# An encoder step on one core: score maxima of the first three tiles ahead of gating, and a tail that begins with the convolution's products

## The chip, the cores and the metric

The kernel runs on one core of a Trainium2 chip. The metric is the device time of one execution in microseconds (us); the time before is the median of three executions.

## The reference

One layer of a streaming encoder reads 2048 prompt frames and 64 sample frames of 1024 channels. Cut to what matters:

```python
h = rmsnorm(x, norm_g)
proj = h @ w_in                                  # 1024 x 2832, all groups at once
q, k = rmsnorm(aq, q_g), rmsnorm(ak, k_g)        # 8 query heads, 2 key heads, width 64
y_attn = band_attention(q, k, v, sinks) * silu(ag)   # chunks of 64, band of 192, ALiBi, sinks
o, state = gla_chunked(gq, gk, gv, log_sigmoid(glr @ w_up + b) / 16)
y_gla = rmsnorm(o, gla_g) * silu(gg)
c = depthwise_conv31(cv * sigmoid(cgl)) + conv_b
y_conv = (silu(layernorm(c)) @ w_pw + b_pw) * silu(cg)
y = concat([y_attn, y_gla, y_conv]) @ w_out
return x + y, new key and value windows, GLA state, conv state
```

All of it is float32. Each large product is made of three products of rounded parts: high by high, high by low and low by high.

## The kernel before

Every engine has a queue of its own, in program order, and the engines meet at semaphores. The order in each queue is written out by hand. Pass A runs over 17 tiles of 128 frames (`t.n` from 0 to 16; the last is the sample) and does attention with its part of the output; pass B runs over 8 blocks of 256 frames and does the gated linear attention, the convolution and their part of the output. The change touches pass A's `body_a` on each engine for the tiles 0 to 2 (`OPENING` holds the tiles 0 and 1), and pass B's end.

Weights come from DRAM as 24 pieces of the input projection and 8 of the output (`A.pieces`, `3 * KT` is the first of the output). ScalarE rounds each to its high part (`split_hi`, L479), VectorE takes the rest as its low part (`split_lo`, L489 for the input, L492 for the output). There are four buffers for the output pieces, so the last four (`3 * KT + STAGES` on) are loaded while tile 0 is worked on. On SyncE's queue these loads stand behind the token load of tile 3 (L531), which waits until ScalarE has squared the tokens of tile 2 (`norm_square`, L650).

In a tile of pass A, TensorE transposes the normalised q and k (L2222), projects part of the next tile (L779), transposes the gates into the bank `T[1]` (L2242), makes scores in two banks (L2257; the third and fourth pair wait for maxima of the first and second), projects on, transposes the softmax (L2292 and L2301), makes the output of the tile before (L795) and the product with v (L2315 to L2317). VectorE takes the low parts of q and k (L1632, L1568) and of v (L1640, two inputs from SBUF), the product of the gate's tanh with the gate (L1655), the maxima of scores plus bias (`scores_max`, L1591), the negatives (L1597), the low part of the x of tile t + 2 (L706), the softmax's sum (L1692) and scale. It gates the output (`y_gate`, L1558), of which ScalarE takes the high part (`y_hi_half`, L1264) and VectorE the low (`y_lo_half`, L1537). For tiles 0 and 1 gating and parts come in the next tile's turn, ahead of its maxima. ScalarE evacuates the projections (L720), takes high parts (L1143, L1272, L1157), the tanh (L1161) and the exponentials (L1184).

The reciprocal norm of x goes a long way: the square on ScalarE, mean and power on GpSimd (`norm_rinv`), a transpose on TensorE into `T[1]` (`spread_rinv`, L668), a copy on ScalarE (`take_rinv`, L673), and GpSimd's multiplication of the x of that tile for pass B (`norm_x`, L679). GpSimd also makes the powers of the norm of q and k (`qk_rinv`, L1005) out of VectorE's sums (`qk_square`, L1578 and L1580).

At the end of pass B, for the last block, VectorE gates the convolution's activation (L1882), updates the GLA state (`state`, L1969), sums the squares of o (L1811), adds the convolution's gate (`y_conv`, L1891) and normalises o (L1829), after GpSimd's power (L1056). ScalarE takes the high part of the convolution's half of y (L1399), VectorE the low (L1848). TensorE transposes o (`o_T`, L2424) and makes four banks of output (`output_end`, L2407) of 12 products each, half from the convolution, half from the GLA group; VectorE adds the residual (L1983), and SyncE stores.

Of the kernel before, what the change touches and what calls it, by code (L numbers as in the profile page):

```python
# [24 lines left out]
ALU = mybir.AluOpType  # L25
# [180 lines left out]
def build(nc, ins, consts, x_T, outs):  # L206
# [13 lines left out]
    with es:  # L220
# [774 lines left out]
        def _(pool):  # L995
# [11 lines left out]
            def body_a(t):  # L1007
# [6 lines left out]
                when(t + 2, norm_rinv)  # L1014
                n = t + 1
                if t.real():
# [6 lines left out]
                    if (t + 2).real():  # L1023
                        pool.wait_ge(x_wide, t.n + 3)
                    else:
                        pool.wait_ge(n_rinv, t.n + 1)
                        pool.wait_ge(x_normed, TILES)
# [6 lines left out]
                if n.real() and n.n > 0:  # L1034
                    qk_rinv(n)
                if n.n == LAST:
# [67 lines left out]
        def _(act):  # L1104
# [9 lines left out]
            def body_a(t):  # L1114
# [23 lines left out]
                if t.real():  # L1138
# [13 lines left out]
                    if t.n == 0:  # L1152
                        take_rinv(t1)
                        act.wait_ge(n_step, 4)
                        evacuate(t1, 0, raw[:, 0:512], bank_of("in", t1.n, 0)[:, :])
# [3 lines left out]
                    act.wait_ge(gate_psum, t.n + 1)  # L1159
                    need(act, y_gated, 2 * t.n)  # L1160
                    nc.scalar.activation(gth[:, :], T[1][:, :], ACT.Tanh, scale=0.5).then_inc(gate_tanh, 1)  # L1161
                    if t.n == 0:
                        split_hi(A, 3 * KT + 2, 3 * KT + STAGES)
                    act.wait_ge(v_lo, t.n + 1)
# [3 lines left out]
                if t.n - 1 in OPENING:  # L1168
                    y_hi_half(t + -1, 0)
                if (t + -1).real():  # L1170
# [35 lines left out]
                if t.real():  # L1206
                    exp_scores(0)
                    exp_scores(1)
                if t.n == LAST:
# [4 lines left out]
                if t.n == 1:  # L1214
                    split_hi(A, 3 * KT + STAGES, len(A.pieces))
                if t.n == 0:
                    norm_square(t + 2)
# [21 lines left out]
                if t.n in OPENING:  # L1239
                    pT_hi(1)  # L1240
                if t1.real():
# [9 lines left out]
                if t.n >= 0:  # L1251
# [262 lines left out]
        def _(dve):  # L1514
# [68 lines left out]
            def body_a(t):  # L1583
# [35 lines left out]
                if t.fixed and t.n == -1:  # L1619
# [3 lines left out]
                    split_lo(A, 2 * KT + STAGES, 2 * KT + STAGES + 2)  # L1623
                    qk_square(B0)
                    split_lo(A, 2 * KT + STAGES + 2, 3 * KT)
# [16 lines left out]
                if t.n - 1 in OPENING:  # L1642
                    y_gate(t + -1, 0)
                    y_gate(t + -1, 1)
                    y_lo_half(t + -1, 0)
                if (t + -1).real():
                    y_lo_half(t + -1, 1)
                if t.real():
# [5 lines left out]
                    dve.wait_ge(gate_tanh, t.n + 1)  # L1654
# [1060 lines left out]
```

## Time and profile before

| | before |
|---|---|
| median of 3 runs | 931.96 us (931.54 to 934.63) |
| profiled execution | 932.18 us, span 930.4 us |
| mean granted TensorE clock | 0.991 |
| TensorE busy | 895.2 us, 96% of the span |
| TensorE weight load busy | 803.9 us, 86% |
| VectorE busy | 783.1 us, 84% |
| ScalarE busy | 481.1 us, 52% |
| GpSimd busy | 215.8 us, 23% |

The span runs from the first to the last instruction of the profiled execution; its own time is 1.8 us longer, for what lies around the span. Busy shares are averages over stages with different limits. In rows, PE is TensorE, PEld its weight load, DVE VectorE, ACT ScalarE, POOL GpSimd and SP SyncE; L12 is line 12 of the kernel before. In rows in order of time the brackets at the end hold the idle time of the engine just before the instruction, and what ended it. Instructions that follow without a gap are merged into one row, with their count.

### The profile page before, as it was taken

How to read it: one execution, taken by the hardware profiler on the slowest of the kernel's cores; microseconds unless marked ns; L12 is line 12 of the kernel's file. 1: busy time of each engine (PE TensorE's matmuls, PEld its weight loads, DVE VectorE, ACT ScalarE, POOL GpSimd, SP SyncE). 2: the span in 40 equal slices, each digit the busy share in tenths (PEclk: the TensorE clock that was granted, in tenths of full speed). 3: DMA queues.
4: the chain of work that ended last, by engine and by line, in shares of the span. 5: the costliest groups of instructions: out<-in, count | busy, mean ns of one | idle time of the engine just before them, and what ended most of it. 6: DMA issues, size and time to landing. Idle time of an engine off the chain costs nothing. (4 is left out here: it accounts for less than half of the span.)

```text
span 930.4 us, 15888 instructions
## 1 busy us (share of the span) xinstructions
PE 895.2 (96%) x5655; PEld 803.9 (86%) x5655; DVE 783.1 (84%) x1896; ACT 481.1 (52%) x1182; POOL 215.8 (23%) x259
## 2 busy tenths in 40 slices
PE   6889999999999999998999999999999999999997
PEld 5777888888888888886998888889999899998985
DVE  6878888888888888889879999888788969788983
ACT  7676667667776666668663261341515224151331
POOL 1432222222221222223022231311202021120310
PEclk9999999999999999999999999999999999999999
DMA  8551322223233333234451221121130302203021
GB/s 285 202 192 69 114 98 108 90 104 114 103 114 114 113 114 98 73 119 135 126 161 51 76 69 63 52 80 57 40 98 1 116 23 69 69 26 111 1 80 59
DMA packets 58062, 88.04 MB, mean 95 GB/s; under 512 B 10080, under 2 KB 34528, under 8 KB 57984
## 3 DMA queue, kind: packets, MB, share of 16 engines
q1 hardware_dynamic: 57984, 87.03, 28.5%
q8 instruction: 45, 0.74, 0.3%
q14 instruction: 33, 0.27, 0.1%
HBM read 60.47 MB, written 26.60 MB: 94 GB/s over the span
## 5 line engine op out<-in xcount | busy, mean ns | idle before, releaser
L1798 DVE SCALAR_TENSOR_TENSOR acc<-ub,cwh,acc 128x256 f32<-128x256 f32 (+1 forms) x480 | 230.3, 539 | 1.5 <-ACT acc L1308 0.7
L779 PE MATMUL J<-whi,xhi 128*128 128x512 f32 (+1 forms) x400 | 148.0, 371 | 7.7 <-DVE wlo L489 7.7
L2200 PE MATMUL J<-xbh,whi 128*128 128x256 f32 (+1 forms) x512 | 152.4, 298 | 0.1
L2200 PE MATMUL J<-xbl,whi 128*128 128x256 f32 (+1 forms) x512 | 146.9, 289 | 1.5 <-DVE xbl L587 1.5
L2200 PE MATMUL J<-xbh,wlo 128*128 128x256 f32 (+1 forms) x512 | 147.7, 289 | 0.0
L779 PE MATMUL J<-wlo,xhi 128*128 128x512 f32 (+1 forms) x400 | 143.4, 359 | 0.0
L779 PE MATMUL J<-whi,xlo 128*128 128x512 f32 (+1 forms) x384 | 137.9, 362 | 0.0
L2200 PEld LDWEIGHTS J<-xbh,whi 128*128 128x128 f32 x512 | 98.8, 193 | 2.2 <-DVE wlo L489 0.8
L2200 PEld LDWEIGHTS J<-xbl,whi 128*128 128x128 f32 x512 | 98.8, 194 | 1.7 <-issue 1.7
L2200 PEld LDWEIGHTS J<-xbh,wlo 128*128 128x128 f32 x512 | 99.0, 193 | 0.5
L779 PEld LDWEIGHTS J<-whi,xhi 128*128 128x128 f32 x400 | 77.5, 194 | 17.8 <-DVE xlo L699 7.2
L779 PEld LDWEIGHTS J<-wlo,xhi 128*128 128x128 f32 x400 | 77.8, 194 | 9.2
L779 PEld LDWEIGHTS J<-whi,xlo 128*128 128x128 f32 x384 | 74.3, 194 | 11.2
L1184 ACT ACTIVATE sc<-sc,nmx 128x192 f32<-128x192 f32 x132 | 58.6, 446 | 9.0 <-DVE nmx L1597 9.0
L795 PE MATMUL J<-whi,yhi 128*128 128x512 f32 x136 | 56.2, 413 | 0.9 <-DVE wlo L492 0.9
L1591 DVE CUSTOM_DVE_ANT_0 sc<-S,bias,sinks 128x192 f32<-128x192 f32 (+2 forms) x132 | 48.8, 406 | 6.3 <-PE S L2257 6.1
L795 PE MATMUL J<-wlo,yhi 128*128 128x512 f32 x136 | 53.1, 390 | 0.0
L679 POOL TENSOR_TENSOR xraw<-xraw,rb 128x1024 f32<-128x1024 f32 x17 | 41.4, 2433 | 43.3 <-ACT rb L673 43.3
L795 PE MATMUL J<-whi,ylo 128*128 128x512 f32 x128 | 50.1, 392 | 0.0
L1056 POOL TENSOR_TENSOR orr<-oms,mhalf 128x8 f32<-128x8 f32 (+1 forms) x9 | 17.8, 1980 | 136.4 <-DVE oms L1821 136.4
L2257 PEld LDWEIGHTS S<-kT,qT 128*128 128x128 f32 x264 | 33.6, 191 | 9.0 <-DVE mx L1591 5.4
L2257 PE MATMUL S<-kT,qT 128*128 128x192 f32 x264 | 35.5, 274 | 6.0 <-DVE mx L1591 4.1
(287 smaller groups left out, 2244.5 us busy)
## 6 DMA issues: line engine op xcount, KB each, us to landing
out<-res SPq DMA_DIRECT2D x60, 256.0 KB, 2.0
x_normed_scratch<-xraw SPq DMA_DIRECT2D x17, 512.0 KB, 2.9
xtok<-in_x_prompt SPq DMA_DIRECT2D x16, 512.0 KB, 3.6
res<-in_x_prompt SPq DMA_DIRECT2D x16, 512.0 KB, 4.5
xraw<-xT SPq DMA_DIRECT2D x15, 512.0 KB, 3.5
xbraw<-x_normed_scratch SPq DMA_DIRECT2D x14, 512.0 KB, 5.0
res<-out SPq DMA_DIRECT2D x14, 512.0 KB, 4.2
wraw<-in_w_in SPq DMA_DIRECT2D x52, 128.0 KB, 2.5
```

Source lines behind the costliest of these rows:

```text
L679: nc.gpsimd.tensor_tensor(xraw[t.par][:, :, :], xraw[t.par][:, :, :], rb[:, :].unsqueeze(1).to_broadcast([P, KT, P]), ALU.mult).then_inc(x ...
L779: last = nc.tensor.matmul(bank[:, 0:width], x[x_slot(ps, t)][:, k, :], w, start=(k == 0 and n == 0), stop=(k == KT - 1 and n == len(produc ...
L795: last = nc.tensor.matmul(bank[:, :], y[:, k, :], w, start=(k == 0 and n == 0), stop=(k == 3 and n == len(products) - 1))
L1056: nc.gpsimd.tensor_tensor(orr[rows, a:e], oms[rows, a:e], mhalf[rows, a:e], ALU.pow).then_inc(go_r, 1)
L1184: last = nc.scalar.activation(unit(u), unit(u), ACT.Exp, bias=nmx[:, u:u + 1], accum_out=esum[:, u:u + 1])
L1591: nc.vector.tensor_tensor_reduce(out=unit(u)[:, cols], in0=S[n % 2][:, c * BAND:(c + 1) * BAND][:, cols], in1=bias[:, n, cols], scale=1.0, ...
L1798: nc.vector.scalar_tensor_tensor(acc[:, j, 0:frames], src, w, acc[:, j, 0:frames], ALU.mult, ALU.add).then_inc(conv_step, 1)
L2200: last = nc.tensor.matmul(bank[:, 0:w], wt, x[:, k, 0:w], start=(k == 0 and m == 0), stop=(k == KT - 1 and m == 2))
L2257: last = nc.tensor.matmul(S[n % 2][:, c * BAND:(c + 1) * BAND], qT[:, n, c, :, :].rearrange("p e q -> p (e q)"), band(t, n // 2, o, c), st ...
```

## The change

In VectorE's queue, the gate product of the tiles 0 to 2 moves behind the maxima and the sink difference. The gating of the tile before moves behind the second negatives in the tiles 1 and 2, and the low halves of its output move behind the gate product. The last four output weights, which stood together in tile 1, are spread: one ahead of the maxima, one behind the second negatives, two behind the gate product. The squares of q and k of tile 0 move one input weight ahead.

In ScalarE's queue, v's high part goes ahead of the reciprocal row and of the evacuation of q in tile 0; the reciprocal row of tile 2 is taken in tile 1, behind v's high part. The tanh and both high halves of the tile before move behind the first two pairs of exponentials in the tiles 1 and 2. The last four output weights stand two ahead of v's copies and two behind the high halves. The square of tile 2's tokens moves behind the second half of the softmax's high parts.

In GpSimd's queue, the reciprocal norm of tile 2 moves behind v's copies and the powers for q and k of tile 1; the copies wait for the multiplication of tile 1's x instead. On TensorE the transpose of tile 2's reciprocal norm moves behind the whole product with v.

At the tail, the last state update moves behind the sums and means of the squares of o, and the output begins with the first two products of each of the convolution's two parts in the first bank, ahead of the transposes of o; three banks instead of two have their convolution half made ahead of the GLA half.

```diff
@@ GpSimd, body_a
-                when(t + 2, norm_rinv)
+                if t.n != 0:
+                    when(t + 2, norm_rinv)
...
-                    if (t + 2).real():
+                    if t.n == 0:
+                        pool.wait_ge(x_normed, 2)
+                    elif (t + 2).real():
                         pool.wait_ge(x_wide, t.n + 3)
...
                 if n.real() and n.n > 0:
                     qk_rinv(n)
+                if t.n == 0:
+                    norm_rinv(t + 2)
@@ ScalarE, body_a
-                    if t.n == 0:
-                        take_rinv(t1)
-                        act.wait_ge(n_step, 4)
-                        evacuate(t1, 0, raw[:, 0:512], bank_of("in", t1.n, 0)[:, :])
                     act.wait_ge(*taken(t, 1))
                     nc.scalar.activation(vcat[t.par][:, :, 0:HD], raw[:, 640:768].rearrange("p (h d) -> p h d", d=HD),
                                          ACT.Copy).then_inc(v_hi, 1)
-                    act.wait_ge(gate_psum, t.n + 1)
-                    need(act, y_gated, 2 * t.n)
-                    nc.scalar.activation(gth[:, :], T[1][:, :], ACT.Tanh, scale=0.5).then_inc(gate_tanh, 1)
+                    if t.n in (0, 1):
+                        take_rinv(t1)
+                    if t.n == 0:
+                        act.wait_ge(n_step, 4)
+                        evacuate(t1, 0, raw[:, 0:512], bank_of("in", t1.n, 0)[:, :])
+
+                    def tanh_of_gate():
+                        act.wait_ge(gate_psum, t.n + 1)
+                        need(act, y_gated, 2 * t.n)
+                        nc.scalar.activation(gth[:, :], T[1][:, :], ACT.Tanh, scale=0.5).then_inc(gate_tanh, 1)
+
+                    if t.n - 1 not in OPENING:
+                        tanh_of_gate()
...
+                    if t.n == 1:
+                        split_hi(A, 3 * KT + STAGES, 3 * KT + STAGES + 2)
...
-                if t.n - 1 in OPENING:
-                    y_hi_half(t + -1, 0)
-                if (t + -1).real():
+                if (t + -1).real() and t.n - 1 not in OPENING:
                     y_hi_half(t + -1, 1)
...
                     exp_scores(0)
                     exp_scores(1)
+                if t.n - 1 in OPENING:
+                    tanh_of_gate()
+                    y_hi_half(t + -1, 0)
+                    y_hi_half(t + -1, 1)
+                if t.n == 1:
+                    split_hi(A, 3 * KT + STAGES + 2, len(A.pieces))
...
-                if t.n == 1:
-                    split_hi(A, 3 * KT + STAGES, len(A.pieces))
-                if t.n == 0:
-                    norm_square(t + 2)
...
                 if t.n in OPENING:
                     pT_hi(1)
+                if t.n == 0:
+                    norm_square(t + 2)
...
-                if t.n >= 0:
+                if t.n > 0:
                     when(t + 2, take_rinv)
@@ VectorE, body_a
-                    split_lo(A, 2 * KT + STAGES, 2 * KT + STAGES + 2)
+                    split_lo(A, 2 * KT + STAGES, 2 * KT + STAGES + 1)
                     qk_square(B0)
-                    split_lo(A, 2 * KT + STAGES + 2, 3 * KT)
+                    split_lo(A, 2 * KT + STAGES + 1, 3 * KT)
...
-                if t.n - 1 in OPENING:
-                    y_gate(t + -1, 0)
-                    y_gate(t + -1, 1)
-                    y_lo_half(t + -1, 0)
-                if (t + -1).real():
+                if (t + -1).real() and t.n - 1 not in OPENING:
                     y_lo_half(t + -1, 1)
+                if t.n == 1:
+                    split_lo(A, 3 * KT + STAGES, 3 * KT + STAGES + 1)
...
-                    dve.wait_ge(gate_tanh, t.n + 1)
-                    nc.vector.scalar_tensor_tensor(gth[:, :], gth[:, :], 1.0, T[1][:, :], ALU.add,
-                                                   ALU.mult).then_inc(gate_ready, 1)
+                    if t.n > 2:
+                        gate_product()
                     scores_max(0)
...
                     scores_neg(1)
+                    if t.n - 1 in OPENING:
+                        y_gate(t + -1, 0)
+                        y_gate(t + -1, 1)
+                    if t.n == 1:
+                        split_lo(A, 3 * KT + STAGES + 1, 3 * KT + STAGES + 2)
...
+                    if t.n <= 2:
+                        gate_product()
+                if t.n == 1:
+                    split_lo(A, 3 * KT + STAGES + 2, len(A.pieces))
+                if t.n - 1 in OPENING:
+                    y_lo_half(t + -1, 0)
+                    y_lo_half(t + -1, 1)
...
-                if t.n == 1:
-                    split_lo(A, 3 * KT + STAGES, len(A.pieces))
@@ VectorE, end of pass B
-                    state(b, 1)
                     o_sums(g)
                     o_means(g)
+                    state(b, 1)
@@ TensorE, body_a
-                when(t + 2, spread_rinv)
+                if t.n != 0:
+                    when(t + 2, spread_rinv)
                 if t.n > 1:
                     out(1)
                 if t.real():
                     pv(1)
+                if t.n == 0:
+                    spread_rinv(t + 2)
@@ TensorE, output_end
+                first = empty_bank("out", b, 0)
+                pe.wait_ge(yc_hi, groups_before(b + 1))
+                output_half(first, 0, 0, (2, 3), parts=(0, 1))
                 o_T(groups(b)[0])
                 pe.wait_ge(yc_lo, groups_before(b + 1))
-                for s in (0, 1):
+                output_half(first, 0, 0, (2, 3), parts=(2,))
+                for s in (1, 2):
                     output_half(empty_bank("out", b, s), s // 2, s % 2, (2, 3))
                 pe.wait_ge(yg_lo, groups_before(b + 1))
-                for s in (0, 1):
+                for s in (0, 1, 2):
                     output_half(bank_of("out", b, s), s // 2, s % 2, (0, 1)).then_inc(slot_done, 1)
-                for s in (2, 3):
-                    output_half(empty_bank("out", b, s), s // 2, s % 2, (2, 3, 0, 1)).then_inc(slot_done, 1)
+                output_half(empty_bank("out", b, 3), 1, 1, (2, 3, 0, 1)).then_inc(slot_done, 1)
```

`output_half` takes a new argument `parts`, which of the three products to make; without it, it makes all three.

## Rows read from the trace of the kernel before

**Rows 1.** Windows of 25 us: busy time by engine, granted clock (PEclk), DMA.

```profile
50.00:75.00 25.00, 21.47 (x117) 17.65 (x118) 20.55 (x59) 19.02 (x50) 6.49 (x8) 0.93 0.39 139
...
100.00:125.00 25.00, 24.95 (x146) 21.65 (x145) 21.11 (x56) 17.00 (x45) 6.50 (x8) 1.00 0.31 106
```

**Rows 2.** Waits of TensorE, 30 to 60 us: total, times, longest (us).

```profile
PE T L2222 <- DVE qkn L1735: 2.1, 1, 2.1
```

**Rows 3.** The same, 60 to 80 us.

```profile
PE S L2257 <- DVE mx L1591: 1.4, 2, 1.3
PE S L2257 <- issue: 1.1, 1, 1.1
PE J L795 <- DVE wlo L492: 0.9, 1, 0.9
```

**Rows 4.** The same, 80 to 100 us.

```profile
PE S L2257 <- DVE mx L1591: 1.3, 2, 1.1
```

**Rows 5.** Windows of one microsecond; the columns of Rows 1.

```profile
34.00:35.00 1.00, 1.00 (x7) 1.00 (x6) 0.95 (x2) 0.97 (x2) 0.00 (x0) 0.50 0.77 78
69.00:70.00 1.00, 1.00 (x3) 0.76 (x3) 0.93 (x2) 1.00 (x3) 0.00 (x0) 0.50 0.49 197
95.00:96.00 1.00, 1.00 (x6) 0.79 (x6) 0.86 (x7) 1.00 (x3) 0.00 (x0) 1.00 1.00 410
916.00:917.00 1.00, 1.00 (x3) 0.75 (x3) 0.43 (x1) 0.00 (x0) 0.00 (x0) 0.50 0.00 0
```

**Rows 6.** VectorE by time: start, us, what, wait before and its releaser.

```profile
28.16 1.41 DVE L489 SCALAR_TENSOR_TENSOR wlo<-res,gain,whi 128x512 fp32r<-128x512 f32 x2
...
39.06 1.81 DVE L1640 TENSOR_TENSOR vcat<-raw,vcat 128x128 fp32r<-128x128 f32 x1 [1.04 <-ACT vcat L1157]
...
48.47 0.30 DVE L1692 TENSOR_TENSOR den<-esum,esink 128x8 f32<-128x8 f32 x1 [1.43 <-ACT esink L1227]
...
60.89 0.29 DVE L1640 TENSOR_TENSOR vcat<-raw,vcat 128x128 fp32r<-128x128 f32 x1
...
63.90 0.76 DVE L1537 TENSOR_TENSOR ylo<-osum,yhi 128x256 fp32r<-128x256 f32 x2 [2.05 <-ACT yhi L1264]
64.69 0.69 DVE L1655 SCALAR_TENSOR_TENSOR gth<-gth,T 128x512 f32<-128x512 f32 x1
65.30 0.41 DVE L1591 CUSTOM_DVE_ANT_0 sc<-S,bias,sinks 128x192 f32<-128x192 f32 x1
...
69.16 1.23 DVE L706 TENSOR_TENSOR xlo<-xraw,xhi 128x1024 fp32r<-128x1024 f32 x1
70.31 2.49 DVE L492 TENSOR_TENSOR wlo<-wraw,whi 128x512 fp32r<-128x512 f32 x4
```

**Rows 7.** GpSimd in order of time.

```profile
38.33 2.40 POOL L679 TENSOR_TENSOR xraw<-xraw,rb 128x1024 f32<-128x1024 f32 x1 [4.89 <-ACT rb L673]
```

**Rows 8.** ScalarE in order of time.

```profile
45.02 1.05 ACT L650 ACTIVATE xtok<-xtok 128x1024 f32<-128x1024 f32 x1
...
54.98 0.59 ACT L1202 ACTIVATE olo<-S 64x512 f32<-64x512 f32 x1 [1.72 <-PE S L2317]
...
58.42 1.16 ACT L1272 ACTIVATE kT<-T 64x128 fp32r<-64x128 f32 x4
```

**Rows 9.** SyncE's DMA issues in order of time.

```profile
46.18 0.33 SPq L531 DMA_DIRECT2D xtok<-in_x_prompt  x1
...
47.03 1.88 SPq L455 DMA_DIRECT2D wraw<-in_w_out  x4
```

**Rows 10.** The wraw buffer's loads issued from 40 to 72 us.

```profile
DMA to landing us min/median/max: 5.3/5.8/6.1
```

**Rows 11.** TensorE at the tail, in order of time.

```profile
913.60 0.66 PE L2424 MATMUL T<-ident,on 128*128 128x128 f32 x4 [2.44 <-DVE on L1829]
```

**Rows 12.** VectorE at the tail.

```profile
909.02 1.15 DVE L1969 SCALAR_TENSOR_TENSOR stp<-stp,dec,T 32x64 f32<-32x64 f32 x4
```

**Rows 13.** ScalarE at the tail.

```profile
912.10 0.63 ACT L1399 ACTIVATE ybc<-cl 128x512 fp32r<-128x512 f32 x1 [3.24 <-DVE cl L1891]
```

More of the change, by code:

```diff
@@ L1641, in body_a, with gate_product @@
                                             f(vcat[t.par][:, :, 0:HD]), ALU.subtract).then_inc(v_lo, 1)
-                if t.n - 1 in OPENING:
-                    y_gate(t + -1, 0)
-                    y_gate(t + -1, 1)
-                    y_lo_half(t + -1, 0)
-                if (t + -1).real():
-                    y_lo_half(t + -1, 1)
+                if (t + -1).real() and t.n - 1 not in OPENING:
+                    y_lo_half(t + -1, 1)
+                if t.n == 1:
+                    split_lo(A, 3 * KT + STAGES, 3 * KT + STAGES + 1)
+                def gate_product():
+                    dve.wait_ge(gate_tanh, t.n + 1)
+                    nc.vector.scalar_tensor_tensor(gth[:, :], gth[:, :], 1.0, T[1][:, :], ALU.add,
+                                                   ALU.mult).then_inc(gate_ready, 1)
                 if t.real():
@@ L2388, in output_end, with output_half @@
             def output_end(b):
+                first = empty_bank("out", b, 0)
+                pe.wait_ge(yc_hi, groups_before(b + 1))
+                output_half(first, 0, 0, (2, 3), parts=(0, 1))
                 o_T(groups(b)[0])
                 pe.wait_ge(yc_lo, groups_before(b + 1))
-                for s in (0, 1):
+                output_half(first, 0, 0, (2, 3), parts=(2,))
+                for s in (1, 2):
                     output_half(empty_bank("out", b, s), s // 2, s % 2, (2, 3))
                 pe.wait_ge(yg_lo, groups_before(b + 1))
-                for s in (0, 1):
+                for s in (0, 1, 2):
                     output_half(bank_of("out", b, s), s // 2, s % 2, (0, 1)).then_inc(slot_done, 1)
-                for s in (2, 3):
-                    output_half(empty_bank("out", b, s), s // 2, s % 2, (2, 3, 0, 1)).then_inc(slot_done, 1)
-            def output_half(bank, i, h, ks, first=2):
+                output_half(empty_bank("out", b, 3), 1, 1, (2, 3, 0, 1)).then_inc(slot_done, 1)
+            def output_half(bank, i, h, ks, first=2, parts=(0, 1, 2)):
                 for k in ks:
@@ L2405, in output_half @@
                     high, low = i * P, y_low_at(i * P)
-                    for m, (at, wt) in enumerate(((high, hi), (high, lo), (low, hi))):
+                    for m in parts:
+                        at, wt = ((high, hi), (high, lo), (low, hi))[m]
                         last = nc.tensor.matmul(bank[:, :], y[:, k % 2, at:at + P], wt,
```

## Prediction

> **What bounds the kernel now.** I read the windows first, then TensorE's waits in the stretches that are not full, then each engine in order of time there and at the tail. The windows show where time can be had at all: from 50 to 75 us TensorE is busy 21.47 of 25 us, from 100 to 125 us 24.95 [rows 1]. Later TensorE is the bound, so that what is won before 100 us is kept to the end: the loads and all engines there follow TensorE's progress. The waits of the first stretches name VectorE nearly every time: 2.1 us for the normalised q and k of tile 0 [rows 2], in tile 1 1.4 us for score maxima, 1.1 before the scores and 0.9 for the last output weight [rows 3], in tile 2 1.3 us for maxima [rows 4].
>
> The single microseconds show a second loss. At 34, 69 and 916 us the granted clock is 0.50, TensorE's lower level of 1.2 GHz [rows 5]. These came after its waits of 2.1 us [rows 2], of 1.4 us in two pieces [rows 3] and of 2.4 us [rows 11]; after the 1.3 us of tile 2 the clock was full at 95 us [rows 4, 5]. The price is in the mean of the 25 us that hold the second one, 0.93 [rows 1]: 25 x 0.07 = 1.75 us of TensorE's work, if TensorE sets the pace then.
>
> VectorE's order in time shows why tile 1 waits: 60.89 low half of v, then gating of tile 0's output, a wait of 2.05 us for ScalarE's high halves of y, their low halves, the gate product, and only at 65.30 the first score maximum [rows 6]. It ended the last of four output weights at 72.80 (70.31 + 2.49) [rows 6], and TensorE's first output product waited for that [rows 3].
>
> **The change, step by step.**
>
> *Tile -1.* The squares of q and k go ahead of one of two weights that stood before them. One such weight takes 1.41 / 2 = 0.7 us [rows 6]. GpSimd's powers, the normalised q and k and TensorE's transposes follow 0.7 sooner. TensorE's wait of 2.1 can take it [rows 2]. The weight that steps back is late by less than this and the next one, for which TensorE waited anyway, is as early as before. Ends: 0, if GpSimd's power is drawn out by VectorE's weights beside it, and 0.7. I take 0.7.
>
> *Tile 0.* Four moves: v's copy goes ahead of the reciprocal norm and of tile 1's q on ScalarE; VectorE's gate product goes behind the maxima; GpSimd copies v before tile 2's norm; and ScalarE's square of tile 2's tokens, 1.05 us plus a short read of the sum [rows 8], leaves the place between the first and second pair of exponentials. The softmax sum on VectorE waited 1.43 us for ScalarE [rows 6], so it comes about 1.0 sooner (at most 1.43, at least 0 if VectorE itself is late). The square now stands ahead of the evacuation of tile 1's gates; behind these ScalarE waited 1.72 us for TensorE [rows 8], which covers it. Sum at tile 1's start: 1.7. Tile 2's reciprocal row moves out of ScalarE's way too, behind v's copy: some 0.3 more for tile 1's keys, so 2.0.
>
> *The queue behind the moved square.* SyncE's token load for tile 3 waits for that square, and behind it stand the residual of tile 0 and the last four output weights: token load at 46.18, first weight at 47.03 [rows 9]. ScalarE went idle at 54.98 - 1.72 = 53.26 [rows 8], after the evacuation of the gates, which I take as long as the copy at 54.98, 0.6; the square comes ahead of it and all is 1.7 sooner, so it ends near 53.26 - 0.6 - 1.7 + 1.15 = 52.1, and the first weight is issued near 53.0. Landing took 5.3 to 6.1 us [rows 10]: 58.3 to 59.1. That is where ScalarE now asks for it.
>
> *Tile 1.* From the start of v's low half to the first maximum there are now 65.30 - 60.89 = 4.4 us [rows 6]. Between them there will be only one weight, 2.49 / 4 = 0.6 [rows 6], but also a new wait. ScalarE's keys end at 59.58 now [rows 8], hence about 57.6; v's high half and the reciprocal row add 0.6, and GpSimd then multiplies tile 2's x from 58.2 on for 2.40 us [rows 7], to 60.6. VectorE comes to v's low half at 60.89 - 2.0 = 58.9. In tile 0 the same instruction, with GpSimd's multiplication beside it, took 1.81 us and ended at 40.87, just after the multiplication's 40.73; alone it took 0.29 [rows 6, 7]. So I count it to end at 60.8, and the first maximum at about 61.45, or 3.85 sooner. From there to the last weight VectorE took 72.80 - 65.30 = 7.5 us [rows 6]. Now two gatings (as long as the low halves of y, 0.76), the gate product (0.69) and the low halves (0.76) come in, 2.2; the first weight (0.6) and x's low half (1.23) go out, 1.8 [rows 6]. So y is ready at about 61.45 + 7.9 = 69.3, 3.5 sooner than 72.80. ScalarE's tanh, its high halves and the last weights lie a little ahead of these by the same count.
>
> TensorE then has nothing for about 2.9 us (its second half of the gates' projection ends near 66.4 by my estimate: maxima 3.85 sooner, 1.4 of waits gone). That is longer than the 2.1 that came before a slow stretch [rows 2, 5], so I count one, 1.7 us. The present one at 69 us is in part hidden by the 0.9 that TensorE waited after it [rows 3]. Sum at tile 2's start: 3.5 - 1.7 = 1.8. Ends: 0, if the new order holds VectorE or ScalarE up by as much as it frees, and 3.5.
>
> The Trainium skill, GPSIMD Engine Reference, section Specifications, says that GpSimd shares its SBUF interfaces with VectorE and contends with VectorE instructions that have two SBUF inputs. It does not say that the later one waits for the other's end; if the two only halved each other's rate, v's low half would take an estimated 0.6 and all behind it would come 1.3 sooner, a time of 926.9. By the row of tile 0 it waits for the end, and by that goes the sum.
>
> *Tile 2.* The same order without weights: both waits for maxima go, 1.3 [rows 4]. VectorE's gate product and low halves then come while TensorE projects the next tile. Ends: 0, if the softmax is late by as much, and 1.3. Sum: 3.1.
>
> *Tail.* VectorE's state update of 1.15 us [rows 12] steps behind the sums of squares, so GpSimd's root and the normalised o come earlier; TensorE no longer waits for these first. It begins the output with four products of the convolution half as soon as ScalarE has its high half, at 912.10 + 0.63 = 912.73 [rows 13]; now it begins at 913.60 with the transposes [rows 11]. All that follows has its inputs by then (the transposes come after four products, the gated part after 14 more), so TensorE runs through: 0.8 sooner. The slow stretch at 916 [rows 5] stays, since a wait of about 1.6 us is left ahead. The last bank, its addition and its store are as now. Ends: 0.4, if the clock rises when it does now, and 2.5, if it does not fall.
>
> *Sum.* 1.8 + 1.3 + 0.8 = 3.9 us from the profiled execution's 932.18 (its span is 930.4), which is 0.2 over the median of the runs: 932.18 - 3.9 = 928.3, and 928.2 with the median in mind. About 0.3%, 2.8 us, is what a measurement of this kernel can tell from no change: below 929.2 is faster, above 934.8 slower.
>
> **Rivals.**
>
> *The clock does not fall in tile 1* (or v's low half isn't held up), 0.22: for it, 1.3 us of waits in tile 2 left the clock up [rows 4, 5]; against it, 2.9 is longer than any of these. The 1.7 stay: 926.5.
>
> *Tile 1 gives back what tile 0 won,* 0.20: VectorE's work ahead of the first output product isn't less than before, only in another order, and each engine hands over to another some ten times. Where ScalarE's high halves come late, VectorE stands behind them with the low halves and the softmax, and TensorE with the output. Then only tile 2 and the tail are left, 2.1: 930.1.
>
> *The tail alone,* 0.07: the maxima weren't what held TensorE, the softmax was: 931.4.
>
> *Slower, through late weights,* 0.04: VectorE's split of the first of the last four weights stands ahead of tile 1's first maximum, ScalarE's half of it ahead of v's copies and all exponentials. By the count it is wanted split by 60.8, so landed by 60.2, and lands by 59.1: 1.1 to spare. Each microsecond more costs one. To end above 934.8 it would have to eat the 3.9 and 2.8 more, landing near 67, 14 us after its issue, where 6.1 was the longest [rows 10]. A landing one or two microseconds late ends in the second rival.
>
> **How the numbers follow.** My forecast, 927.2 to 929.4, has 0.47. The likeliest time is 928.2. The range reaches from 926.0 (clock up in tile 1, and part of the tail's) to 930.6 (tile 1 giving all back, and a little of tile 2): about 0.1 is left out on each side. Faster: 0.45 of the forecast, the 0.22 and nothing of the rest, 0.67. Slower: 0.04, and 0.01 for what I don't see, 0.05. Same: 0.28.
>
> **What would show it.** Right: first transposes of tile 0 near 32.0 instead of 32.7; the softmax sum of tile 0 near 46.6; v's low half of tile 1 near 1.9 us long; first maximum near 61.5; one TensorE wait of 2 to 3 us ahead of the first output product, with clock 0.50 behind it; no waits for maxima in tile 2; output at the tail from 912.8 less what was won before. Wrong: ScalarE waiting for a weight's DMA in tile 1, a wait of TensorE for the softmax in tile 0 or 1 that isn't there now, or a span that is shorter only behind 900 us.

## Result and profile after

The changed kernel took 925.15 us, the median of four runs (925.01 to 925.71), against 931.86 for the kernel before beside it: a ratio of 0.9929, 95% interval 0.9912 to 0.9946. So it is 6.7 us faster (5.0 to 8.2 by the interval), where 3.9 were forecast, and it ends 0.85 us below the range. A second measurement later gave 0.9929 again (0.9916 to 0.9941). The profiled execution took 925.71 us, with a span of 923.9 (930.4 before).

TensorE's waits after the change, in the stretches of [rows 2 to 4] (waited for: us in total, times, longest):

```profile
PE T L2270 <- ACT rb L673: 1.3, 2, 0.8
PE T L2250 <- DVE qkn L1763: 1.3, 1, 1.3
PE S L2285 <- DVE kT L1583: 0.6, 1, 0.6
...
PE J L795 <- DVE ylo L1552: 2.4, 1, 2.4
...
PE S L2343 <- DVE px L1741: 0.5, 1, 0.5
```

The wait for the normalised q and k is 1.3 us in place of 2.1. In tile 1 the three waits have become the one of 2.4 us ahead of the first output product, and tile 2 has none for maxima. The single microseconds that answer to [rows 5] (busy us of each engine, then the granted clock, DMA share, GB/s; the output at the tail is now at 909 to 912):

```profile
34.00:35.00 1.00, 0.82 (x7) 0.58 (x6) 0.39 (x1) 0.93 (x4) 0.00 (x0) 1.00 0.48 53
69.00:70.00 1.00, 1.00 (x4) 0.81 (x3) 0.45 (x3) 0.46 (x4) 0.00 (x0) 0.50 0.00 0
95.00:96.00 1.00, 1.00 (x10) 0.91 (x8) 0.97 (x3) 0.82 (x3) 0.00 (x0) 1.00 0.00 0
...
911.00:912.00 1.00, 1.00 (x6) 0.79 (x5) 0.30 (x2) 0.63 (x1) 0.00 (x0) 1.00 0.00 0
```

Two of the three slow stretches (granted clock 0.50) are gone, at 34 us and at the tail; the one in tile 1 is still there. Each of the two profiles has two more in the middle, near 440 and 529 us before and near 416 and 526 us after, which the forecast did not look at. VectorE, GpSimd and ScalarE in order of time, where [rows 6 to 8] stood:

```profile
45.38 0.16 DVE L1720 TENSOR_TENSOR den<-esum,esink 128x8 f32<-128x8 f32 x1
...
57.75 1.94 DVE L1655 TENSOR_TENSOR vcat<-raw,vcat 128x128 fp32r<-128x128 f32 x1
...
60.32 0.42 DVE L1606 CUSTOM_DVE_ANT_0 sc<-S,bias,sinks 128x192 f32<-128x192 f32 x1
...
67.09 0.76 DVE L1552 TENSOR_TENSOR ylo<-osum,yhi 128x256 fp32r<-128x256 f32 x2
```

```profile
57.15 2.39 POOL L679 TENSOR_TENSOR xraw<-xraw,rb 128x1024 f32<-128x1024 f32 x1 [4.75 <-ACT rb L673]
```

```profile
57.35 1.29 ACT L479 ACTIVATE whi<-wraw 128x512 fp32r<-128x512 f32 x2 [0.28 <-DMA wraw<-in_w_out]
```

v's low half takes 1.94 us and ends at 59.69, just after GpSimd's multiplication (57.15 + 2.39 = 59.54). ScalarE waits 0.28 us for a weight. At the tail, TensorE before (the row ahead of [rows 11]), then after:

```profile
909.16 1.99 PE L2468 MATMUL T<-cth,params 128*128 128x256 f32 x8 [1.23 <-DVE cth L1882]
```

```profile
905.17 1.99 PE L2503 MATMUL T<-cth,params 128*128 128x256 f32 x8 [1.23 <-DVE cth L1910]
908.89 0.47 PE L2442 MATMUL J<-whi,ybc 128*128 128x512 f32 x1 [1.72 <-ACT ybc L1414]
...
909.89 0.60 PE L2459 MATMUL T<-ident,on 128*128 128x128 f32 x4
```

Cut at six of TensorE's own instructions, every trace gives a ledger of the span. "Start" ends at tile 0's transposes of q and k, "tile 0" at those of tile 1, "1a" at tile 1's first output product, "1b" at tile 2's transposes, "tile 2" at tile 3's; "middle" runs to the last block's products of `cth` (the convolution's gated activation), "tail" from there to the end. An asterisk marks a slow stretch (left out in the middle).

```
kernel                     start  tile 0    1a     1b    tile 2  middle   tail
before                     32.73  23.10*  17.11*  8.47   27.04   800.71  21.21*
before, again (e1)         32.63  21.81   17.11  10.00*  27.09   800.80  21.21*
squares only (e13)         31.74  21.83   17.11   8.43   27.06   801.39  21.21*
changed                    31.09  21.60   15.26  10.03*  25.71   801.48  18.75
changed, again (e10)       31.70  21.61   15.26   8.79   26.00   802.22  18.75
head only (e2)             31.75  21.59   15.24   9.97*  25.70   801.99  21.21*
```

In the profiled execution of before the stretch of tile 1 lies in 1a, which takes the same 17.11 us without it; in the other three that have one there it comes behind the first output product, in 1b, where it costs 1.2 to 1.6 us.

### The profile page after: what moved, and what is told of

It is laid out like the page before. It is cut to its first block and busy times, and to the rows that moved or that the text cites. A ratio compares the mean times of both kernels' runs of the same rounds, so it can differ in the third digit from the quotient of the medians.

```text
span 923.9 us, 15888 instructions
## 1 busy us (share of the span) xinstructions
PE 890.1 (96%) x5655; PEld 800.9 (87%) x5655; DVE 784.4 (85%) x1896; ACT 481.6 (52%) x1182; POOL 215.7 (23%) x259
## 5 line engine op out<-in xcount | busy, mean ns | idle before, releaser
L2389 PE MATMUL J<-whi,xbh 128*128 128x272 f32 x136 | 40.0, 294 | 0.0
L2389 PE MATMUL J<-whi,xbl 128*128 128x272 f32 x136 | 39.3, 289 | 0.0
```

The source lines that it names most:

```text
L2389: last = nc.tensor.matmul(bank[:, 0:B.widths[1]], x[:, k, at:at + P], wt, start=(k == 0 and m == 0), stop=(k == KT - 1 and m == 2))
```

## Experiments

**The kernel before once more (e1), the head alone (e2), the tail alone (e3).** e2 is the changed kernel with the tail of before, e3 the kernel before with the changed tail: the state update one place later, and

```diff
+                first = empty_bank("out", b, 0)
+                pe.wait_ge(yc_hi, groups_before(b + 1))
+                output_half(first, 0, 0, (2, 3), parts=(0, 1))
                 o_T(groups(b)[0])
...
```

> The kernel before, profiled once more. Theory A (the first loads fell otherwise in the two executions): the powers of tile 0's q and k, the wait for its first transposes (32.73 and 31.09 us in the two profiles) and the end of GpSimd's first multiplication differ by some tenths between two profiles of this same kernel too, up to 0.9. Theory B (the reordering gave all 1.6 us): first transposes within 0.2 of 32.73. For the clock: if slow stretches belong to the waits, they lie at 34, 68 and 914 us again.

> The change without its two edits at the tail. Theory A (the tail gave 2.5, since a slow stretch of the clock went with it): 4.0 to 4.4 us under the kernel before, 927.5 to 927.9, and a slow stretch at the tail as before. Theory B (the tail gave the 0.8 of its earlier start, the rest lies in the first tiles): 5.9 under, 926.0.

> The kernel before with the two edits at the tail alone. Theory A: 2.5 us under the kernel before, 929.4, with no slow stretch behind 900 us. Theory B: 0.8 under, 931.1, and the slow stretch still there.

e1 took 932.44 us, e2 928.39 (0.9950, 0.9936 to 0.9964), e3 929.83 (0.9969, 0.9958 to 0.9981), beside 932.66. Theory A of e2 and of e3 holds: e2 keeps the slow stretch at the tail, e3 has none there. Head 4.3 and tail 2.8 us add up to 7.1, the whole being 6.7; within the intervals the two gains simply add. e1, the same program as before, shows what the forecast had no view of:

```profile
32.63 0.63 PE L2222 MATMUL T<-ident,qkn 128*128 128x128 f32 x4 [2.11 <-DVE qkn L1735]
...
71.55 0.47 PE L795 MATMUL J<-whi,yhi 128*128 128x512 f32 x1 [2.50 <-DVE wlo L492]
71.86 0.57 PE L795 MATMUL J<-wlo,yhi 128*128 128x512 f32 x1
72.22 0.63 PE L795 MATMUL J<-whi,ylo 128*128 128x512 f32 x1
```

```profile
46.85 0.17 DVE L1692 TENSOR_TENSOR den<-esum,esink 128x8 f32<-128x8 f32 x1 [0.44 <-ACT esink L1227]
```

```profile
34.00:35.00 1.00, 1.00 (x11) 1.00 (x10) 0.97 (x2) 0.95 (x3) 0.00 (x0) 1.00 0.00 0
...
73.00:74.00 1.00, 1.00 (x4) 0.74 (x3) 1.00 (x5) 0.71 (x3) 0.00 (x0) 0.50 0.00 0
```

The same wait of 2.11 us is not followed by half clock at 34 us this time. TensorE, faster in tile 0 and 1, then waits 2.50 us for the last weight and not the 0.92 of [rows 3], and the slow stretch comes behind that, where a product takes 0.63 us in place of 0.39. The sum of tile 0, 1a and 1b is 48.68 us in the one, 48.92 in the other. The first transposes come within 0.1 us of 32.73, as theory B had it; but e3, e5 and e6, with the same head, have them at 31.56, 32.25 and 32.22, so the spread of theory A is there too.

**What the tail is worth without its products (e6), and the clock without the tail's order (e5).** e6 is the kernel before with the state update alone moved, e5 the kernel before with

```diff
             def output_end(b):
+                first = empty_bank("out", b, 0)
+                for n in range(9):
+                    nc.tensor.matmul(first[:, :], xbh[:, n % KT, 0:P], whi[:, W_OUT:W_OUT + 512], ...)
```

> The kernel before with the last state update behind the sums and means of the squares of o, and the output's order as before. Theory A (any work of TensorE that begins some 0.8 us sooner leaves the clock up): 0.8 to 2.5 under the kernel before. Theory B (what counts is the four products ahead of the transposes): 0.0 to 0.8 under, since the transposes of o, and with them all products, begin when o is normalised, about 912.7 instead of 913.6; the slow stretch stays.

> The kernel before, with nine products of finished operands added on TensorE in the output, ahead of the transposes of o (their results are overwritten; the order of all else is that of before). TensorE then does something in the 2.4 us in which it waited for o. Theory A (the tail's gain in the changed kernel is for the larger part the slow clock stretch behind that wait, worth 1.7 us): the granted clock stays at 1.00 behind the place, the last products end 1.7 us sooner although no work was moved, and the time is 1.2 to 2.0 us under the kernel before, a ratio of 0.9979 to 0.9987. Theory B (the gain is the earlier start of the output): no gain, a ratio of 1.000 or a little above, with the slow stretch there or not.

e6: 929.93 us (0.9977, 0.9967 to 0.9986). e5: 930.56 (0.9981, 0.9971 to 0.9991). TensorE in e6, then in e5:

```profile
908.63 1.99 PE L2468 MATMUL T<-cth,params 128*128 128x256 f32 x8 [1.23 <-DVE cth L1882]
912.19 0.66 PE L2424 MATMUL T<-ident,on 128*128 128x128 f32 x4 [1.57 <-DVE on L1829]
912.98 0.53 PE L2407 MATMUL J<-whi,ybc 128*128 128x512 f32 x1
913.32 0.62 PE L2407 MATMUL J<-wlo,ybc 128*128 128x512 f32 x1
```

```profile
911.02 2.44 PE L2392 MATMUL J<-whi,xbh 128*128 128x512 f32 x9
913.81 0.66 PE L2428 MATMUL T<-ident,on 128*128 128x128 f32 x4 [0.35 <-DVE on L1829]
914.41 0.50 PE L2411 MATMUL J<-whi,ybc 128*128 128x512 f32 x1
914.75 0.39 PE L2411 MATMUL J<-wlo,ybc 128*128 128x512 f32 x1
```

From the `cth` products to the transposes e6 needs 3.56 us where the kernel before needs 4.44, and its products still take 0.62: its tail is 20.53 us, 0.7 shorter. e5 moves nothing, its transposes come 4.43 us behind `cth`, its products take 0.39, and its tail is 19.67 us, 1.5 shorter. So theory A of e5 holds: at the tail the clock is the larger part. One thing stays open: by the times e6 gains nearly as much as e3 (0.9977 and 0.9969, overlapping). Its profiled execution, 930.95 us, had a mean clock of 0.993; seven of its twelve runs had 0.994, which is about one slow stretch less (e9 with one has 0.998, e15 with none 1.000), and took 929.6 to 930.0. If that was the stretch at the tail, moving the state update is enough to be rid of it in most executions; whether the four products ahead of the transposes are needed is not shown.

**The squares of q and k (e4, e13), and the clock of tile 0 (e14).** e4 undoes that move in the changed kernel, e13 makes it alone in the kernel before, e14 adds nine products ahead of tile 0's transposes in the kernel before.

```diff
-                    split_lo(A, 2 * KT + STAGES, 2 * KT + STAGES + 2)
+                    split_lo(A, 2 * KT + STAGES, 2 * KT + STAGES + 1)
                     qk_square(B0)
-                    split_lo(A, 2 * KT + STAGES + 2, 3 * KT)
+                    split_lo(A, 2 * KT + STAGES + 1, 3 * KT)
```

> The changed kernel with one edit undone: VectorE's squares of q and k of tile 0 stand behind two weights again, as before the change. Theory A (the move of the squares is worth what TensorE waited less there, 2.1 us of the kernel before against 1.3 of the changed one; the rest of the 1.64 us by which the changed kernel's first transposes came sooner is how the first loads happened to land): TensorE's wait for the normalised q and k is 2.1 us again, and the time is 0.7 to 0.9 us above the changed kernel's, a ratio to the kernel before of 0.9932 to 0.9942. Theory B (the whole 1.64 us came of the move): 1.6 us above it, a ratio of 0.9942 to 0.9950. Theory C (what tile 0 wins is swallowed by the waits of tile 1, as in my second rival): no difference, 0.9925.

> The kernel before with one edit of the change alone: VectorE's squares of q and k of tile 0 ahead of one weight. Theory A (the shorter wait of 1.4 us instead of 2.1 leaves TensorE's clock up, and both are kept): first transposes of tile 0 near 31.4 us, no slow stretch between 31 and 38 us, 21.8 us from them to those of tile 1, and the time 0.7 to 2 us under the kernel before, a ratio of 0.978 thousandths short of one at most: 0.9978 to 0.9992. Theory B (in the old order tile 1 gives back what the clock saves in tile 0: of five executions with the old head tile 1 took 27.1 us in the two with a fast tile 0 and 25.6 in two of the three with a slow one): only the 0.7 of the shorter wait is left or not even that, 0.9990 to 1.0000.

(The range meant there is 0.9978 to 0.9992; the figure ahead of it is a slip.)

> The kernel before, with nine products of finished operands added on TensorE ahead of tile 0's transposes, in the 2.1 us of the wait for the normalised q and k (results overwritten; nothing is moved). Theory A (the slow stretch at 34 us is a cost of its own, 1.3 us of tile 0): no slow stretch there, tile 0 takes 21.8 us in place of 23.1, and the time is 0.5 to 1.3 us under the kernel before, 0.9986 to 0.9995. Theory B (tile 1 gives it back, in its wait for the last weights): tile 0 takes 21.8 us, tile 1 27.1, and the time is that of the kernel before, 0.9995 to 1.0003.

e4: 926.55 us (0.9936, 0.9919 to 0.9952), start 32.15, wait 2.11, a slow stretch back at 33 to 36 us: theory A, though the interval of the ratio holds all three. e13: 930.22 us (0.9985, 0.9976 to 0.9994), a gain of 1.4 us, as theory A had it. Its trace:

```profile
31.74 0.63 PE L2222 MATMUL T<-ident,qkn 128*128 128x128 f32 x4 [1.41 <-DVE qkn L1735]
...
53.57 0.63 PE L2222 MATMUL T<-ident,qkn 128*128 128x128 f32 x4
...
70.68 0.47 PE L795 MATMUL J<-whi,yhi 128*128 128x512 f32 x1 [2.50 <-DVE wlo L492]
70.98 0.40 PE L795 MATMUL J<-wlo,yhi 128*128 128x512 f32 x1
```

The wait is 1.41 and tile 0 at full clock; here even the 2.50 us in tile 1 leave the clock up (0.40 a product). e14: 931.08 us (0.9989, 0.9979 to 0.9999); tile 0 takes 21.87 us and 1b 10.02, as theory B had it, yet the time is nearer to A. Between those two it settles nothing.

Over all traces, waits of 2.10 to 2.11 us ahead of tile 0's transposes were followed by half clock in four of six, waits of 1.27 to 1.43 in none of ten. The mean start is 32.28 us with the old order (before, e1, e3, e5, e6) and 31.41 with the new one (ten traces): 0.9, with some overlap (31.56 in e3, 31.75 in e2). Left out are e4 (old order, 32.15) and e14 (old order with the wait filled, 31.36).

**ScalarE's square back (e9), and the changed kernel again (e10).**

```diff
+                if t.n == 0:
+                    norm_square(t + 2)          # between tile 0's pairs of exponentials
...
-                if t.n == 0:
-                    norm_square(t + 2)          # behind the second half of P's high parts
```

> The changed kernel with ScalarE's square of tile 2's tokens back between tile 0's two pairs of exponentials. Theory A (my step of tile 0: the square held up the softmax by 1.0 us): the softmax sum of tile 0 comes 1.0 us later than in the changed kernel, tile 1 begins 0.7 to 1.1 us later, and the time is 0.4 to 1.1 us above it, a ratio of 0.993 to 0.9945. Theory B (the square at its new place holds up the token load and behind it the last four weights, for which ScalarE waits in tile 1, so that the move gives back what it wins): the weights land about 3 us sooner, ScalarE no longer waits for one, and the time is that of the changed kernel or up to 0.5 us under it.

> The changed kernel once more, beside the next three. Theory A (the time is settled by the order of the work, and where slow clock stretches fall adds about 1 us either way): a ratio to the kernel before of 0.992 to 0.994, first transposes of tile 0 between 31.0 and 32.0 us after a wait of 1.2 to 1.5 us, a slow stretch behind the wait ahead of tile 1's output product, and none behind the wait at the tail. Theory B (the 6.7 us were in part one lucky place of the clock): 0.994 to 0.996, with a slow stretch back at 34 us or at the tail.

e9: 925.20 us (0.9927, 0.9914 to 0.9941); e10: 925.77 (0.9929). VectorE, ScalarE and SyncE in e9:

```profile
44.19 1.22 DVE L706 TENSOR_TENSOR xlo<-xraw,xhi 128x1024 fp32r<-128x1024 f32 x1
45.33 0.16 DVE L1720 TENSOR_TENSOR den<-esum,esink 128x8 f32<-128x8 f32 x1
```

```profile
44.60 0.19 ACT L1242 ACTIVATE esink<-sdif 128x8 f32<-128x8 f32 x1
```

```profile
43.46 1.97 SPq L455 DMA_DIRECT2D wraw<-in_w_out  x4
```

The softmax sum comes 14.29 us after tile 0's first transposes, as in the changed kernel (45.38 - 31.09): VectorE has its own queue until then and ScalarE's exponential is done at 44.79. Theory A falls. The weights are issued 8.0 us sooner (51.47 in the changed kernel) and ScalarE waits for none, but 1a is 15.25 us as before. The move brings and costs nothing that these runs could show.

**GpSimd's multiplication in tile 1 (e8, e11).** e8 holds it back past v's low half and the first weight; e11 puts it behind tile 0's low half of y.

```diff
+                if t.n == 0:
+                    pool.wait_ge(A.wlo, 3 * KT + STAGES + 1)
                 if t.n >= -1:
                     when(t + 2, norm_x)
```

```diff
+                if t.n == 1:
+                    pool.wait_ge(A.y_lo, 2)
+                    norm_x(t + 1)
...
-                if t.n >= -1:
+                if t.n >= -1 and t.n != 0:
                     when(t + 2, norm_x)
```

> The changed kernel, with GpSimd's multiplication of tile 2's x (2.39 us at 57.15) held back until VectorE is through with v's low half and the first weight in tile 1. Theory A (the 1.94 us of v's low half are a wait for GpSimd's multiplication, and they lie on the path to the first maximum): v's low half takes 0.3 us, the first maximum and the low half of y come 1.3 to 1.6 us sooner, TensorE's wait ahead of the output falls from 2.44 us to about 1, the time is 1.3 to 1.6 us under the changed kernel, and up to 3.2 if the clock then does not fall behind the shorter wait: a ratio of 0.989 to 0.991. Theory B (v's low half is slow for another reason, such as its own operands): it stays at 1.9 us and the time as it is, 0.9925. Theory C (GpSimd's later multiplication brings tile 2's projections late instead): v's low half is short, and TensorE waits for x of tile 2 by about as much, 0.9925 or above.

> The changed kernel, with GpSimd's multiplication of tile 2's x (2.4 us) moved behind tile 0's low half of y, out of all of tile 1's maxima and weights. When it was only held back past v's low half, the 1.65 us of delay went over to VectorE's next short instruction beside it (a negated maximum of 0.17 us took 1.68). Theory A (that second delay is why the first one's going brought nothing): both are gone, the low half of y comes 1.0 to 1.6 us sooner and the time is 1.0 to 1.6 us under the changed kernel, a ratio of 0.990 to 0.9915. Theory B (ScalarE's wait for the second of the last weights, which lands near 59.1 us, binds the exponentials and y as well): v's low half takes 0.3 us, no negated maximum is long, but y and the time are as in the changed kernel, within 0.5 us. Theory C: the delay goes over once more, to the low half of x or the softmax of tile 1 beside the multiplication's new place, and tile 2 begins no sooner.

e8: 925.38 us (0.9923, 0.9909 to 0.9937). e11: 926.04 (0.9935, 0.9922 to 0.9947). VectorE, GpSimd and ScalarE in e8:

```profile
58.23 0.29 DVE L1657 TENSOR_TENSOR vcat<-raw,vcat 128x128 fp32r<-128x128 f32 x1
...
59.49 0.41 DVE L1608 CUSTOM_DVE_ANT_0 sc<-S,bias,sinks 128x192 f32<-128x192 f32 x1
...
59.95 1.68 DVE L1614 TENSOR_SCALAR nmx<-mx 128x2 f32<-128x2 f32 x1
```

```profile
59.20 2.40 POOL L679 TENSOR_TENSOR xraw<-xraw,rb 128x1024 f32<-128x1024 f32 x1 [6.32 <-DVE wlo L492]
```

```profile
59.09 0.63 ACT L479 ACTIVATE whi<-wraw 128x512 fp32r<-128x512 f32 x1 [1.02 <-DMA wraw<-in_w_out]
```

v's low half is 0.29 us: its 1.94 were the multiplication. But the next instruction that it holds is a negated maximum, 0.17 us of work that lasts until 61.63 (59.20 + 2.40 = 61.60), while a maximum that reads PSUM (59.49) ran beside it unharmed. TensorE's wait ahead of the output product is 2.68 us here, so nothing of theory A's time came. e11 moves it on, and VectorE and TensorE show where the delay went:

```profile
67.43 1.22 DVE L706 TENSOR_TENSOR xlo<-xraw,xhi 128x1024 fp32r<-128x1024 f32 x1
69.30 1.62 DVE L1723 TENSOR_TENSOR den<-esum,esink 128x8 f32<-128x8 f32 x1 [0.65 <-ACT esink L1243]
```

```profile
67.65 3.25 POOL L679 TENSOR_TENSOR xraw<-xraw,rb 128x1024 f32<-128x1024 f32 x1 [3.69 <-issue]
```

```profile
71.57 0.90 PE L2323 MATMUL T<-ident,sc 128*128 128x128 f32 x4 [0.96 <-DVE sc L1728]
```

It is the softmax sum of tile 1 now (0.17 us alone, 1.62 here), and TensorE waits 0.96 for what follows: theory C. 1a falls by 0.35 and 1b, with full clock, is 10.37. v's low half ends 1.6 us sooner and y only 0.35; ScalarE's wait for the second weight, 1.28 us in e11, holds part of the rest (theory B): in e12, where it is gone, 1a is 0.39 shorter again. What holds what is left isn't shown.

**Filling tile 1's wait (e7, e15), and all three edits (e12).** e7 and e15 are one kernel, the changed one with nine products ahead of `out(0)`; e12 has these, e11's move, and the second weight's high half behind v's copies.

```diff
+                if t.n == 1:
+                    spare_bank = empty_bank("outa", 0, 0)
+                    for n in range(9):
+                        nc.tensor.matmul(spare_bank[:, :], xhi[t1.par][:, n % KT, :], whi[:, 0:512], ...)
                 if t.n == 1:
                     out(0)
```

> The changed kernel, with nine products of finished operands added on TensorE in tile 1, ahead of the first output product (their results are overwritten), where TensorE waits 2.44 us for VectorE's low half of y. Theory A (that wait is followed by the slow stretch of 68 to 71.5 us, and the stretch costs 1.0 to 1.7 us that the rest of the kernel does not get back): the clock stays at 1.00 at 68 us, tile 2 begins 1.0 to 1.7 us sooner than in the changed kernel, and the time is as much under it, a ratio to the kernel before of 0.9907 to 0.9915. Theory B (behind the wait TensorE is held by VectorE's and ScalarE's work on the last weights and on y, so that a faster TensorE waits there instead): the clock is 1.00 but tile 2 begins as in the changed kernel, a ratio of 0.9925.

> The changed kernel with three edits together: the multiplication of tile 2's x behind tile 0's low half of y; ScalarE's high half of the second of the last weights behind v's copies, so that its landing near 59.1 us no longer holds the copies; and nine products of finished operands added on TensorE ahead of tile 1's first output product (results overwritten), which alone kept the clock at 1.00 there. Theory A (the three waits are one chain, and each hides the other): y is 0.8 to 1.5 us sooner than in the kernel with the nine products alone, and the time is 0.5 to 1.5 us under that one's 0.9913, a ratio of 0.9897 to 0.9908. Theory B (what is won in tile 1 is given back when tile 2 waits for the softmax or at the passage to the second pass, where the changed kernel gave back 0.9 us): 0.991 to 0.992.

> The changed kernel with nine added products ahead of tile 1's first output product once more. Theory A (the added products keep the clock up in tile 1, and that shortens the kernel): a ratio of 0.9905 to 0.992, under the two measurements of the changed kernel (0.9929 and 0.9929). Theory B (a slow stretch that does not fall in tile 1 falls later at one of the places where TensorE waits, near 416, 438 or 525 us, or the passage to the second pass gives it back): 0.992 to 0.994.

e7: 924.30 us (0.9913, 0.9899 to 0.9927); e15: 925.18 (0.9926, 0.9912 to 0.9939); e12: 925.27 (0.9928, 0.9915 to 0.9940). TensorE in e7:

```profile
65.64 2.20 PE L2358 MATMUL J<-whi,xhi 128*128 128x512 f32 x9
68.28 0.47 PE L795 MATMUL J<-whi,yhi 128*128 128x512 f32 x1 [0.44 <-DVE ylo L1552]
68.59 0.40 PE L795 MATMUL J<-wlo,yhi 128*128 128x512 f32 x1
```

The clock stays up and 1b is 8.78 us (twice), 1.25 less. The time gained is 0.3 to 1.5 us by the two ratios, whose intervals overlap the changed kernel's: a version that beats both is not shown. In e12 1a is 14.51, the best of all, and 1b 9.95, since the softmax sum is held for 1.74 us: what it won it gave back.

## Why the prediction was wrong

Two steps failed, both of the clock: the slow stretch at the tail that was to stay, and the one charged to tile 1. Of the terms for the order alone, only tile 0's was wrong.

**Where time can be had** held: all that was won lies ahead of tile 3 and at the tail. **Tile −1** (0.7): right, 0.9 in the mean and 0.7 of TensorE's wait.

**Tile 0** (1.0): wrong in its reason. In executions at full clock the tile takes 21.8 us before and 21.6 after, so the order brings 0.2; the square that I moved out of the exponentials cost nothing (e9). The 1.43 us of [rows 6] belonged to an execution whose TensorE was slow at 34 us; in e1 that wait is 0.44, and the softmax sum comes 14.22 us after the tile's transposes, in the changed kernel 14.29. It was my lower end, "at least 0 if VectorE itself is late", that came true. In the profiled pair tile 0 is 1.50 us shorter all the same, 1.3 of it the slow stretch: the shorter wait of tile −1 leaves the clock up. I had the row [rows 5] and did not draw that. That tile 0 gave about the 1.0 forecast is luck.

**The queue behind the moved square:** the weights came about when ScalarE asked for them (0.28 us late in the changed kernel, at most 1.4 in the others, e7). The count was right; ScalarE's wait for a weight, which I had named as a sign of being wrong, did appear, but it didn't decide the time (e9, where none was late, has the same 1a).

**Tile 1:** the count was right nearly to the tenth. 1a is 17.11 to 17.13 us in all seven traces with the old order and 15.23 to 15.30 in eight with the new one (all but e11 and e12): 1.86, where 1.8 was forecast (y 3.5 sooner, 1.7 of it won ahead of tile 1). v's low half took 1.94 (1.9 forecast), the wait 2.44 (2.9). The step that failed is "so I count one, 1.7 us". The kernel before pays for such a stretch too, at 34 us, with the one in tile 1 hidden in 1a (before, e6), or behind its own wait of 2.50 us, in 1b (e1, e5); in e3 it pays for both. I charged the new order in full and credited the old one with nothing. In the means 1b costs 0.4 us more, not 1.7 (9.40 over five traces, before, e1, e3, e5 and e6; 9.76 over the changed kernel, e10, e2, e9 and e8). In the profiled pair the charge was nearly right, 1.56: it is too large as a mean, and the pair beat the forecast elsewhere (see the sum).

The Trainium skill, GPSIMD Engine Reference, section Specifications, lists contention of GpSimd with VectorE instructions that have two SBUF inputs or run in a two-port mode; the trace agrees for v's low half, which has two (which mode the negated maximum ran in, no run shows). The choice of the row over a halved rate was right: the later of the two instructions waits for the other's end (0.29 us became 1.94, 0.17 became 1.62). Behind VectorE's low half of x it was GpSimd that waited: 3.25 us in place of 2.40 (e11).

**Tile 2** (1.3): right, 1.33 in the pair, 1.09 from e1 to e10.

**Tail** (0.8): the term for the order was right, the first product 3.72 us after the `cth` products and not 4.44, 0.7 sooner. What failed is "The slow stretch at 916 [rows 5] stays, since a wait of about 1.6 us is left ahead". After 1.72 us of wait the clock stayed at 1.00 in all ten traces with the new tail, which makes the 2.5 us that stood there as the far end. e5 shows 1.5 of it with nothing moved but the wait filled. This is the largest error: the tail gave 2.46 in the pair, 1.7 more than forecast.

**Sum.** By the ledger, as profiled (forecast in brackets): start -1.64 (-0.7), tile 0 -1.50 (-1.0), 1a -1.85 (-1.8), 1b +1.56 (+1.7), tile 2 -1.33 (-1.3), middle +0.77 (0), tail -2.46 (-0.8): -6.45 (-3.9). The middle is 800.7 and 800.8 us in before and e1, and 801.4 to 802.2 in the other four rows above. These four have a slow stretch near 417 us that the two lack, but that doesn't decide it: e15, with no slow stretch at all, has 801.59, and e8, with one near 417 us, 800.92. Over all traces the middle is 800.6 to 801.6 us with the old tile 1 (seven, mean 801.0) and 800.7 to 802.2 with the new (ten, mean 801.3), so most of the pair's 0.77 is spread between executions; what makes the spread stays open.

The gain isn't just a lucky clock. Over the runs whose clock is on record the kernel before has a mean clock of 0.987 to 0.996 and the changed one of 0.993 to 1.000; at the same mean clock the changed one is shorter by some 6 us (0.993: 931.8 in 26 runs and 926.0 in 2; 0.994: 931.4 in 4 and 925.4 in 4), though the stretches need not lie at the same places.

Of the **rivals**, "the clock does not fall in tile 1" came true in e10 and not in the profile of the changed kernel, at the same time to within 0.7 us. The second and third are refuted by e2, the fourth by ScalarE's 0.28 us.

## What to carry to other kernels

When half-clock stretches show in a profile, compare several executions of the same kernel before pricing a wait: cut each into segments, and charge or credit a stretch to both kernels alike. A wait that is shortened can be worth more than what it is shortened by (the tail: 0.7 us by order, 2.5 in all), and filling one with idle products can win time with nothing moved (e5); for the other two fillings (e7 with e15, e14) a gain is not, or barely, shown. Before moving an instruction out of an engine's queue, look whether the engine that waits for it has a full queue of its own in an undisturbed execution.

## What the runs showed that was not expected

The length of the last wait alone does not decide whether the clock falls. At the tail 1.57 us were followed by half clock (e6), 1.72 were not (ten traces); in tile 1 2.3 to 2.5 us were in e1 and the changed kernel, and were not in e10, e11 and e13.

GpSimd's 2.4 us multiplication takes some 1.5 us from VectorE wherever in tile 1 it was put, from an instruction of 0.17 us as from one of 0.29. Instructions with an operand in PSUM passed beside it: the maxima in e8, and in the changed kernel the keys' last low part, 0.29 us at 57.43, between the multiplication's start and v's low half.
